# A two-block transformer on one core: attention maps one step deeper, token-major expert-down, and a top-k look-up in PSUM

## The reference

```python
# first block, twice (l = 0: attention, l = 1: short convolution)
mod = silu(c) @ ada_w[l] + ada_b[l]               # six vectors: shift, scale, gate, twice
h  = x * (1 + sc1) + sh1;  hc = ctx * (1 + csc1) + csh1
y  = concat(diff_attention(...), gqa_attention(...)) @ w_out   # 4 heads of two maps; 8 heads
x  = layer_norm(ALPHA * x + g1 * y);  x = layer_norm(ALPHA * x + g2 * relu(h2 @ w1)**2 @ w2)
# diff_attention: o = (softmax(s0) - lam * softmax(s1)) @ v;  o = rms_norm(o, subln_g) * 0.8
# second block
merged = sigmoid(ga) * retention(...) @ w_a + sigmoid(gb) * moba_attention(...) @ w_b
x = x + merged @ w_out
# 16384 experts of one neuron; 8 heads pick 16 each by two sub-keys of 128
top 16 of each half, top 16 of the 256 sums, experts = i1 * 128 + i2, gates = softmax
x = x + sum_k gate_k * gelu(h . u[expert_k]) * v[expert_k]
```

## Time and profile before

| | |
|---|---|
| Median of 3 runs | 2227.98 us (2224.99 to 2231.34) |
| Profiled execution | 2228.36 us, span 2226.3 us |
| Busy: PE, weight loads, DVE, ACT, POOL | 2022.3, 1738.3, 1157.8, 899.9, 1015.6 us |
| Granted clock of TensorE, mean | 0.958 of full speed |
| Weights read | 335 MB, 151 GB/s over the span |
| Largest groups in the chain that ended last | PE L421 21%, L1001 11%, L760 8%, L403 8%, L1007 5% |

### The profile page before, as it was taken

One profiled execution on the slowest core, in us unless ns is written; L12 is line 12 of the kernel. 1 busy time (PEld: TensorE's weight loads), 2 busy tenths in 40 slices (PEclk: granted clock), 3 DMA queues, 4 the chain that ended last, 5 costly groups with the idle time before them and its releaser, 6 DMA issues.

```text
span 2226.3 us, 35967 instructions
## 1 busy us (share of the span) xinstructions
PE 2022.3 (91%) x13082; PEld 1738.3 (78%) x13082; DVE 1157.8 (52%) x2334; ACT 899.9 (40%) x1378; POOL 1015.6 (46%) x421
## 2 busy tenths in 40 slices
PE   7998777879988979996998897998999999999998
PEld 1644333679988879996877677997999999888887
DVE  1123433153342543343075112699999996666666
ACT  1213443144434235443444214554444444444443
POOL 0434444134436324443834004797666665444443
PEclk9999988899999999998999998999999999999999
DMA  7544343335534435543522243554444445555554
GB/s 261 165 138 158 127 150 134 124 117 183 180 132 134 149 105 181 185 152 118 175 90 100 76 132 108 176 179 137 141 150 144 151 142 180 188 187 187 186 188 157
DMA packets 92840, 337.67 MB, mean 152 GB/s; under 512 B 10272, under 2 KB 11600, under 8 KB 92240
## 3 DMA queue, kind: packets, MB, share of 16 engines
q1 hardware_dynamic: 90432, 329.29, 44.5%
q10 hardware_dynamic: 2320, 7.15, 0.8%
HBM read 335.34 MB, written 1.06 MB: 151 GB/s over the span
## 4 chain that ended last, share of the span: by engine, by line
PE 69%; DVE 24%; DMA 2%; ACT 2%; issue 2%; POOL 1%; ACTq 0%; SPq 0%; DVEq 0%
PE ps L421 21%; PE ps L1001 11%; PE ps L760 8%; PE ps L403 8%; PE ps L1007 5%; DMA ring<-stream 2%; PE ps L734 2%; PE ps L504 2%; PE ps L439 2%; DVE arena L1419 2%; PE ps L617 1%; DVE hot_hi_a L1963 1%; PE ps L579 1%; DVE hot_lo_a L1964 1%; DVE hot_hi_b L1963 1%
## 5 line engine op out<-in xcount | busy, mean ns | idle before, releaser
L363 POOL TENSOR_TENSOR ring_lo<-ring,ring_hi 128x1024 fp32r<-128x1024 f32 x417 | 1015.4, 2440 | 1198.9 <-ACT ring_hi L357 1198.3
L357 ACT ACTIVATE ring_hi<-ring 128x1024 fp32r<-128x1024 f32 x556 | 586.9, 1057 | 498.8 <-DMA ring<-stream 493.9
L421 PE MATMUL ps<-h_lo,ring_hi 128*128 128x256 f32 x2176 | 311.4, 287 | 7.2 <-DVE h_lo L1646 7.2
L421 PEld LDWEIGHTS ps<-h_lo,ring_hi 128*128 128x128 f32 x2176 | 285.9, 195 | 8.7 <-DVE h_lo L1646 8.7
L1001 PE MATMUL ps<-e_pair,ring_hi 128*128 128x512 f32 x1024 | 256.4, 392 | 0.0
L1998 DVE TENSOR_TENSOR e_pair<-arena,e_pair 128x256 fp32r<-128x256 f32 x128 | 174.9, 1367 | 107.7 <-ACT e_pair L1290 107.2
L1001 PEld LDWEIGHTS ps<-e_pair,ring_hi 128*128 128x128 f32 x1024 | 184.2, 189 | 32.9
L403 PE MATMUL ps<-arena,ring 128*128 128x256 f32 (+1 forms) x720 | 184.8, 417 | 15.4 <-DVE arena L1864 5.2
L403 PEld LDWEIGHTS ps<-arena,ring 128*128 128x128 f32 x720 | 142.1, 198 | 54.5 <-issue 23.0
L421 PE MATMUL ps<-arena_r,ring_hi 128*128 128x256 f32 x1024 | 155.3, 296 | 31.1 <-DVE arena_r L1642 29.6
L421 PE MATMUL ps<-late_r,ring_hi 128*128 128x256 f32 x1152 | 166.9, 288 | 7.4 <-DVE late_r L1642 7.4
(11 more groups left out here) (245 smaller groups left out, 2516.2 us busy)
## 6 DMA issues: line engine op xcount, KB each, us to landing
ring<-stream SPq DMA_DIRECT2D x628, 512.0 KB, 3.3
arena<-decay ACTq DMA_DIRECT2D x1, 1536.0 KB, 6.6
cst<-consts ACTq DMA_DIRECT2D x1, 1036.0 KB
resid<-x_t ACTq DMA_DIRECT2D x1, 1024.0 KB
arena<-ctx_t ACTq DMA_DIRECT2D x1, 1024.0 KB
late<-bias_rows ACTq DMA_DIRECT2D x1, 1024.0 KB, 5.2
out<-resid ACTq DMA_DIRECT2D x2, 512.0 KB, 2.6
late<-lam_in ACTq DMA_DIRECT2D x1, 128.0 KB
```

The source lines that it names most:

```text
L357: act.activation(ring_hi[:, s, :], ring[:, s, :], ACT.Copy).then_inc(hi_ready, 1)
L363: eng.tensor_tensor(ring_lo[:, s, :], ring[:, s, :], ring_hi[:, s, :], ALU.subtract).then_inc(lo_ready[s], 1)
L421: m = pe.matmul(ps[:, bank, 0:T], w[:, kc * P:(kc + 1) * P], x[:, kc, :], start=begin, stop=w is w_lo and kc == KC - 1)
```

## The change

- The early rows are unrolled: four banks (4, 5, 0, 1) and four row buffers; the columns of row g - 1 come after the rows of g. The bias row comes after them all. The modulated x and context are each computed half by DVE and half by ACT, x first; the projections wait for x only, tile 2 for the context. ACT writes the bias row out after that and waits for it there.
- `attention` runs two steps over the number of maps. The values come a step later, ahead of the transposes; the late units lie before or after the transposes, the columns ahead. ACT copies a transposed map before it splits units. DVE norms map m - 1 before its columns or its `ring_lo`.
- The head norm runs within the sixteen maps: squares in map 1, sums with the columns of map 4 in bank 7, roots in map 5, the spreading in maps 10 and 14 into bank 6. The last four late units are part of the loop.
- `hot`, `pick_u` and a copy of `iota16` lie in PSUM during the top-k search.
- Expert-down has the tokens as stationary operand and streams 512 features of v, twelve matmuls into four banks, on top of the residual, which 16 matmuls with the identity put there first. DVE and ACT each copy two banks out, SP and ACT store them, token-major.

```diff
+EARLY_BANKS = (4, 5, 0, 1)
+        early_row = area(14336, EARLY_ADA // 4, 512)
+        hot = ps[:, 0:4, :].rearrange("p b (n a) -> p (b n) a", a=TOPK)
+        pick_u = ps[:, 7, P:2 * P].bitcast(U32)
+        iota16_ps = ps[:, 7, 0:TOPK]
...
+            for g in range(EARLY_ADA // 4):
+                early_rows(g)
+                if g == 0:
+                    pe.wait_ge(inputs, 16 * 7)
+                else:
+                    early_columns(g - 1)
+            early_columns(EARLY_ADA // 4 - 1)
+            bias_row()
...
-            def attention(n_maps, scores, keys_of, at_t, values, between=None):
-
-                for m in range(n_maps + 1):
+            def attention(n_maps, scores, keys_of, at_t, values, early=None, late_part=None):
+
+                for m in range(n_maps + 2):
                     if m < n_maps:
                         scores(m)
-                    if between is not None:
-                        between(m)
-                    if m >= 1:
+                    if early is not None:
+                        early(m)
+                    if m >= 3 and m % 2 == 1:
+                        pe.wait_ge(emptied[4], fills[4].now())
+                        pe.wait_ge(emptied[5], fills[5].now())
+                        values(m // 2 - 1)
+                    if 1 <= m <= n_maps:
...
-                        if k % 2 == 1:
-                            pe.wait_ge(emptied[4], fills[4].now())
-                            pe.wait_ge(emptied[5], fills[5].now())
-                            values(k // 2)
+                    if late_part is not None:
+                        late_part(m)
...
             attention(8, scores_a, lambda k: 4, lambda k, kt: attn[:, k % 2, kt * P:(kt + 1) * P], values_a,
-                      lambda m: ada_between(m + 1, 28))
+                      lambda m: ada_pair(m + 1) if m % 2 == 0 else ada_columns() if m < 9 else None,
+                      lambda m: ada_pair(m + 1) if m % 2 == 1 and m < 9 else None)
...
+            def after_b(m):
+                ada_pair(m + 10)
+                if m in (10, 14):
...
             attention(16, scores_b, lambda k: 4, lambda k, kt: attn[:, k % 2, kt * P:(kt + 1) * P], values_b,
-                      lambda m: ada_between(m + 10, 26))
-
-            late_unit(LATE_ADA - 4, False)
-            late_unit(LATE_ADA - 3)
-            pe.wait_ge(squared, n_squared.add())
...
+                      lambda m: ada_columns(m == 4) if m % 2 == 0 else None, after_b)
...
+            def resid_rows():
+
+                for tt in range(2):
+                    for half in range(2):
+                        b = 2 * tt + half
+                        start_fill(b)
+                        for q in range(4):
+                            pe.matmul(ps[:, b, q * P:(q + 1) * P], resid[:, 4 * half + q, tt * P:(tt + 1) * P],
+                                      const("ident"), start=q == 0, stop=False, skip_group_check=True)
...
+                def product(w, x, tt, begin=False, end=False):
+                    for half in range(2):
+                        m = pe.matmul(ps[:, 2 * tt + half, :], x[:, e % 4, tt * P:(tt + 1) * P],
+                                      w[:, half * 512:(half + 1) * 512], start=False, stop=end, skip_group_check=True)
...
+                product(w_hi, e_hi, 0, begin=True)
+                product(w_hi, e_hi, 1)
                 pe.wait_ge(e_lo_ready, at_trip(i, TRIP, e + 1))
+                product(w_hi, e_lo, 1)
+                product(w_hi, e_lo, 0)
                 wait_unit_lo(u, i)
+                product(w_lo, e_hi, 0, end=last)
+                product(w_lo, e_hi, 1, end=last)
...
             def attention(n_maps, exp_of, evac_of, between=None):
...
-                    if between is not None:
-                        between(m)
                     if m >= 1:
                         k = m - 1
                         b = 4 + k % 2
                         act.wait_ge(full[b], drains[b].add())
                         evac_of(k, b)
+                    if between is not None:
+                        between(m)
...
+            for c, src in enumerate((resid, z)):
+                for kc in range(4, KC):
...
+                m.then_inc(h_act, 1)
+            act.wait_ge(row_ready, 1)
+            act.dma_start(bias_rows, rowbuf[0:8, :]).then_inc(row_out, 16)
             act.wait_ge(row_out, 16)
...
+            for tt in range(2):
+                act.wait_ge(full[2 * tt + 1], mark["experts"][2 * tt + 1])
+                act.activation(rows_out[:, tt, 512:], ps[:, 2 * tt + 1, :], ACT.Copy).then_inc(act_rows, 1)
...
                     if m < n_maps:
                         max_of(m)
                     q = None if ada_map is None else ada_map(m)
+                    if m >= 1:
+                        norm_of(m - 1)
                     if q is not None and q % 2 == 0:
-                        late_columns(MID_ADA // 4 + q // 2 - 1)
+                        late_columns(MID_ADA // 4 + q // 2 - 1, q == 14)
```

More of the change, by code:

```diff
@@ L479, in _, with early_rows @@
-            ada_rows(FIRST_UNIT["ada0"], between=bias_row)
-            with rolled(pe, EARLY_ADA // 8 - 1, [(fills[b], 1) for b in (4, 5, 6, 7)]) as i:
-                ada_rows(FIRST_UNIT["ada0"] + 8, i)
-            def ada_columns():
-                pe.wait_ge(emptied[7], fills[7].now())
+            def early_rows(g):
+                b = EARLY_BANKS[g]
+                start_fill(b)
+                for k4 in range(4):
+                    w = unit(FIRST_UNIT["ada0"] + 4 * g + k4)
+                    for k2 in range(2):
+                        kc = 2 * k4 + k2
+                        m = pe.matmul(ps[0:2, b, :], cact[:, kc, :], w[:, k2 * 512:(k2 + 1) * 512],
+                                      start=kc == 0, stop=kc == KC - 1)
+                        if k2 == 0:
+                            m.then_inc(units_begun, 1)
+                m.then_inc(full[b], 1)
+                fills[b].add()
@@ new lines, in early_columns @@
+            def early_columns(g):
+                pe.wait_ge(emptied[EARLY_BANKS[g]], fills[EARLY_BANKS[g]].now())
+                b = 6 + g % 2
+                start_fill(b)
+                for q in range(4):
+                    m = pe.matmul(ps[:, b, 2 * q:2 * q + 2], early_row[0:2, g, q * P:(q + 1) * P],
+                                  const("ident")[0:2, 0:2], start=True, stop=True)
+                m.then_inc(full[b], 1)
+                fills[b].add()
+            for g in range(EARLY_ADA // 4):
[4 more added lines that the diff above has]
+                    early_columns(g - 1)
@@ L1044, in drain @@
                 act.activation(dst, ps[:, b, 0:n], func, **kw).then_inc(emptied[b], 1)
-            with rolled(act, EARLY_ADA // 8, [(drains[4], 1), (drains[5], 1)]):
-                for g in range(2):
-                    act.wait_ge(full[4 + g], drains[4 + g].add())
-                    act.activation(mod_row[0:2, g, :], ps[0:2, 4 + g, :], ACT.Copy).then_inc(emptied[4 + g], 1)
+            for g in range(EARLY_ADA // 4):
+                act.wait_ge(full[EARLY_BANKS[g]], 1)
+                act.activation(early_row[0:2, g, :], ps[0:2, EARLY_BANKS[g], :], ACT.Copy).then_inc(
+                    emptied[EARLY_BANKS[g]], 1)
+            drains[4].add()
+            drains[5].add()
             n_norm, n_var, n_act_step = Count(), Count(), Count()
@@ L2016, in _ @@
                     expert_lo(8 + e, i, i * 8 + 8 + e)
[L2018 to L2027 removed]
+            for tt in range(2):
+                dve.wait_ge(full[2 * tt], mark["experts"][2 * tt])
+                dve.tensor_copy(rows_out[:, tt, 0:512], ps[:, 2 * tt, :]).then_inc(dve_rows, 1)
         @block.gpsimd
@@ L2068, in _ @@
                 load(v, v % RING)
+            for tt in range(2):
+                sp.wait_ge(dve_rows, tt + 1)
+                sp.dma_start(out[tt, :, 0:512], rows_out[:, tt, 0:512]).then_inc(stored, 16)
 def _constants():
```

233 lines of the change are left out of this document (101 added, 132 removed).

## The result

The changed kernel takes 2168.76 us (median of four runs, 2162.47 to 2177.43) against 2229.34 beside it: a ratio of 0.9734, 95% interval 0.9696 to 0.9771. Forecast were 2166.2 us, range 2145 to 2192. The execution that was profiled is the slowest of the four: 2177.43 us, span 2175.2, mean clock 0.955, so 8.7 us of what it shows are its own. One run of that second timing, 2809.15 us at a granted clock of 0.661, is in a slow state and is left out of its median.

What follows compares the result with a forecast made beforehand. The prediction took the expert stage as bound by TensorE's matmuls and the first block's attention by the order of hand-overs. Its terms summed to -62.2 us from 2228.4, giving 2166.2 us, range 2145 to 2192.

Steps and rivals of the forecast that it cites:

- First modulation, -4.5: Early modulation units: waits and idle loads -4.0, input x first -2.0, bias row's landing +1.5; sum -4.5 us, bounds -7 and -1.
- Attention of the eight maps, -5: First block's first eight maps: column waits and some copies go, VectorE's split ends later in even steps; -5 us, bounds -9 and -1.
- The sixteen maps, their tail and the head norm, -25.5: First block's later maps: copy waits go, head norm moves inside, -21.5; clock -4; sum -25.5 us, bounds -36 and -12.
- Second attention, -7: Second block's attention: 12.0 us of norm and copy waits go, 5.0 given back to the gate tile's drain; bounds -10 and -3.
- Look-up, -10.8: Top-k search: with operands in PSUM, VectorE's operations shorten and TensorE's whole 10.8 us wait goes; bounds -12 and -3.
- Expert-down, -9.3 and +3.7: Expert stage: twelve matmuls at 2.72 us an expert instead of 2.794, -9.3 us; 16 residual matmuls add 3.7.
- Tail, -3.8: After the last matmul: one bank copy and the store, 3.8 us in place of 7.6; bounds -4.5 and -2.
- the ring: Rival, chance 0.17: four unit slots set the attention's pace if landings are 1.5 us later; +16 us, 2182.
- The look-up was not slow: Judges a rival, chance 0.09: look-up operations stay slow or collisions only move, 8 of 10.8 us lost; 2174.
- a matmul did cost more than its columns: Judges a rival, chance 0.05: expert-down matmuls cost only their columns, so the twelve save nothing; 2175.5 us.
- the clock came back: Judges a rival, chance 0.11: attention's clock returns to its upper level and slots never bind; 9 and 5 us more, 2152.
- No weight load was bare: Judges a rival, chance 0.04: expert-down's second weight load is not hidden; at 0.06 us each, 30 us lost, 2258.

Runs made afterwards that it cites:

- that second timing: The changed kernel timed again with no edit, as the mark for the runs beside it: 2169.31 us, ratio 0.9751 to the kernel before.

## Why the prediction was right, and where it was not

The time came out 2.6 us from the forecast, but that closeness is partly luck: the eight maps were forecast 17 us too well, and the sixteen maps, the second attention and the look-up together 10 to 13 us too badly.

*First modulation, -4.5: sized wrongly twice.* Up to the first projection it brings 6.5 to 9.6 us between any two profiles (predicted 6), and 2.2 us of waits for splits come behind it (predicted 1.5). In the timings it is worth 0.9 and 2.7 us. The 3 to 6 us between are not found: in the run of this part alone the profile keeps 8.6 us up to the first map and 9.0 to the end, but it is the fastest of its twelve executions. The projections that are 3.5 us longer in both profiles of the changed kernel are not so in four others with the same program up to there. This stays open.

*Attention of the eight maps, -5: wrong in sign.* It is +9 to +16 in the profiles, +9 to +14 in the timings. The step that failed is "in even steps the split by VectorE now ends behind the norm (1.2 us later...), so I give only -5". It looked at even steps alone. In the odd steps the pair went behind the transposes, and there nothing covers the maxima of one double map and the norm of the one before it, 5.8 us from the scores (209.43 to 215.23); up to 4.9 us lay bare. Two of the 5.8 are the operation of 2.19 us that ended only with POOL's second subtraction, a collision that the sum had for the look-up and not here. And it priced idle time at its own length, while what followed the longer waits ran at the lower level.

*The sixteen maps, their tail and the head norm, -25.5: the mechanism right, the size short.* 142.0 us became 113.3 and 108.8 in two profiles, so -28.7 and -33.2 (three more kernels with this order of the stage: 109.0 to 114.8 us). The copies' waits went whole. The head norm within the maps is 5.6 to 7.6 of it.

*Second attention, -7: too small.* -10.0 in the traces, -12 timed. The wrong term is the 0.6 us that each period should have given back to the gate tile, 5.0 in all. TensorE does wait for that drain, but at the value products, 2.2 us in five times, and did so before: 2.3 of the 4.7 us that the prediction read as waits for the copy were for it (L1044). So of 12.0 us of waits 8.3 went and 3.7 are left, and none were added; the rest of the 10.0 is mostly busy time, 51.7 us in the stage before and 49.3 after.

*Look-up, -10.8: too small.* -14.5 and -13.1. The operations take 2.3 us as forecast, and as forecast a neighbour got slower (L1957, 1.1 us twice). By the traces the term left out is what the wait cost besides itself, slow matmuls behind it, and one wait of 1.1 us for POOL.

*Expert-down, -9.3 and +3.7: right.* 2.72 us an expert, 3.5 us for the residual (1818.71 to 1822.21).

*Tail, -3.8.* 4.5 us from the last matmul in place of 3.8, so -3.1: I counted one copy and ACT has two, with a store each.

Of the rivals, the ring didn't set the pace, neither as the change stands nor with one unit moved forward. ACT does wait for landings, 35.4 us in seventeen times in the sixteen maps, but TensorE for POOL's low part only 3.8. The look-up was not slow, a matmul did cost more than its columns, and the clock came back only in the sixteen maps of some executions (0.88 and 0.92 against 0.87 before). No weight load was bare.

With my own terms put right (-1 to -3, +12, -30, -10 to -12, -13 to -14.5, -5.6, -3) the sum is -51 to -56, near the -57 that the two timings of the changed kernel give.

## What to carry to other kernels

Before a pipeline is made a step deeper, write down for both kinds of step what the engine does between asking for a tile and needing it: the order that brought most of 29 us where the maxima and the norm take VectorE under 2 us lost some 12 where they take 5.8. Look also at what another engine does at that moment, since 2 of the 5.8 us are an operation of 0.16 us that ended only with POOL's. Price a wait with what runs behind it, since here long waits left the next matmuls at the lower level. An early gain seen at a landmark must also be timed, because nearly 8 us at the first projection were worth 1 to 3 in the whole.

## What the hardware showed that I had not expected

- A VectorE operation on one number per row of the statistics (L1604), 0.16 us elsewhere, took 2.19 us from 211.53, ending at 213.72 just as POOL's two subtractions in a row ended (209.06 + 4.64 = 213.70). It did so in each of the four odd steps, and lies in the path of the normed map. The Trainium skill (GPSIMD Engine Reference, 2. Architecture) says that POOL's SBUF read port is shared with DVE; the trace agrees so far as the two end within 0.02 us of each other all four times.
- VectorE reading one operand from PSUM and writing PSUM took 2.295 us for 2048 elements where the same operation in SBUF took 3.9, and the 128-element shifts, with their output in PSUM, 0.295 in place of 1.31. Both were measured with POOL at work on the splits; neither was run without it.
- After 10.79 us of standing, TensorE's next eight matmuls took 2.06 us in place of 1.12, and after 4.89 us those of the next pair stayed near 1.05 to 1.20 in place of 0.62. By the Trainium skill (TensorE: Matmul & The Clock Gate, What's actually happening) the throttled clock is the default and activity releases it; the trace agrees, with 1.20 us after the long wait and 0.63 after one of 0.91.
